# A two-layer hybrid attention and recurrence trunk on one core: output projection's o half scaled as it leaves its slot, value products in other banks, sums' inverses by GpSimd's queue, and several orders of waits and loads

## The chip, the cores and the metric

The program runs on one core of one Trainium2 chip. The time is that of one whole inference step (two layers) in device microseconds, from launch to end; lower is better. Inside the core TensorE (PE) multiplies matrices, VectorE (DVE) and ScalarE (ACT) do elementwise work, GpSimd (POOL) does a few sums and issues DMAs, and SyncE (SP) issues most DMAs. Each engine runs its own instructions in order; semaphores tie them together.

## What is computed

There are 1074 columns of tokens (16 meta tokens, 1024 of a prompt, 32 of a running stream, 2 of padding). Cut to what matters here, a layer of the reference is:

```
z = rmsnorm(x, norm_mix_g) @ w_in                  # -> c_q, c_kv, k_r, x_r, g_r
y = h(x_r) * gelu(g_r)                             # conv, gated recurrence (scan over time)
q = rmsnorm(c_q, q_norm_g) @ w_uq ; ckv = rmsnorm(c_kv) ; kpe = rope(k_r)
k_nope, v = split(ckv @ w_ukv)                     # 8 heads, 64 + 32 rotary columns
o = softmax(mask(q k^T)) v                         # chunk-causal
h = x + concat(rmsnorm(o, attn_out_g), rmsnorm(y, lru_out_g)) @ w_out
x = h + square(relu(rmsnorm(h, norm_mlp_g) @ w_up)) @ w_down
```

## The kernel before

Everything lies transposed: features in the 128 partitions, the 1074 tokens in the free dimension, in three chunks of 358 columns. Each fp32 operand is split into a high and a low part (`xh`, `xl`, `whi`, `wlo`), and each product is three passes of them. A product of 8 blocks of 128 features is so 72 matmuls of 358 columns; one of 4 blocks (the halves of the output projection) is 36.

**Slots and units.** PSUM's banks 0 to 2 and 3 to 5 are two slots. Products are numbered as units `U_...` and take the slots in turn. `take(u)` makes TensorE wait until unit u-2 has been read out of the slot; `READ` says by which semaphore. The sums of squares that the norms need (`sum_of`) go to banks 6 and 7.

**Weights.** 102 blocks of weights a layer come by SP's queue into two buffers `raw0`, `raw1`. `split(b)` stands on ScalarE (which copies `whi`, once the last unit on block b-2 is done) and on VectorE (which subtracts for `wlo`, and counts `w_lo`); TensorE waits for `w_lo`. `load(b)` waits until block b-2 is split.

**The order of a layer.** Four products for the conv's input (`U_XR`), four for the gelu branch (`U_GR`) with the recurrence's gates between them (`gates`), latent, rotary key and query products, `U_UQ` (queries), `U_K`, ten value products of 128 keys each (`U_V`), with the row maxima of head 0 between them, then 8 heads of 19 steps. After them the output projection: 8 units `U_OY` for the y half, then 8 units `U_OO` for the o half, then 4 groups of 16 MLP units. All orders of the five engines are written out by hand; semaphores count per layer.

**Attention.** The scores of step gi need the shifted maxima of their head (`mt`, high and low), which DMAs put into rows of `qe` or `qo`: SP those of the prompt (`aug`), GpSimd those of the few other tokens (`few_shifts`, `aug_few`). `low_parts` (GpSimd) makes the low halves. The softmax sums leave by `srow`, go through DRAM to 16 partitions (`comp`), are inverted by VectorE (`invert`), go back through DRAM and are spread over 64 partitions each (`rc`); `divide(j)` multiplies two heads' o by them. For the last pair this happens while the y half runs.

**The output projection.** `add_y(i)` adds unit `U_OY[i]` to x and frees its slot. The root mean square of o (`rs`) comes from squares made by ScalarE and added by GpSimd (`sum_squares`), summed by TensorE after `U_OY[4]`, then `root` (ScalarE) and `rstd` (VectorE, a reciprocal). Before the change each `o[j]` is multiplied by `rs`, its high half `oh` made by ScalarE and its low half `ol` by VectorE, and only then do the products of the o half start.

## Time and profile before

| | |
|---|---|
| runs | 2770.68 us median of 3 (2768.52 to 2771.31) |
| the profiled execution's own time | 2772.09 us |
| its span, first to last instruction | 2769.9 us |
| mean granted TensorE clock | 0.987 |
| busy: PE / DVE / ACT / POOL | 96% / 47% / 29% / 12% |
| DMA, mean | 52 GB/s |

A busy engine is one with an instruction in flight. The granted clock is a share of TensorE's full speed; 1.00 is 2.4 GHz, and about 0.5 is 1.2 GHz.

### The profile page before, as it was taken

The numbers are of one execution on the slowest core, as the hardware profiler recorded it, in microseconds if no ns is written. First come the engines' busy times: TensorE is split into PE (matmuls) and PEld (weight loads), VectorE is DVE, ScalarE is ACT, GpSimd is POOL, SyncE is SP. The second block draws the span as 40 slices with busy tenths as digits, with TensorE's granted clock in tenths as the row PEclk, the third lists the DMA queues.
The fourth block names the chain that finished last, engine by engine and source line by source line (L and its number), as shares of the span: only waits on it lengthen the run. The fifth ranks groups of instructions, "written<-read, shape, count | busy, mean of one in ns | idle before, by whom it ended". The sixth has DMA issues, their size and how long they took to land.

```text
span 2769.9 us, 37058 instructions
## 1 busy us (share of the span) xinstructions
PE 2668.4 (96%) x15742; PEld 2570.7 (93%) x15742; DVE 1297.4 (47%) x1425; ACT 811.4 (29%) x1240; POOL 327.9 (12%) x192
## 2 busy tenths in 40 slices
PE   6999999999999999999989999999999999999996
PEld 5999977899999999999989998778999999999995
DVE  5899667463223223223368995665632222221323
ACT  3254255442112112022214434552320120210221
POOL 0024144120000000000201223421200000000001
PEclk9999999999999999999999999999999999999998
DMA  3112101211111111111221121012111111111111
GB/s 122 54 61 65 56 16 34 80 46 46 46 46 46 45 41 46 46 47 54 79 73 54 54 80 32 10 41 94 46 46 40 45 46 46 47 43 42 46 46 64
DMA packets 43409, 143.57 MB, mean 52 GB/s; under 512 B 8256, under 2 KB 9376, under 8 KB 43248
## 3 DMA queue, kind: packets, MB, share of 16 engines
q1 hardware_dynamic: 38432, 128.65, 14.2%
q0 software_dynamic: 3232, 6.99, 0.7%
q10 hardware_dynamic: 1584, 5.54, 0.5%
q8 instruction: 132, 2.16, 0.3%
q14 instruction: 29, 0.24, 0.0%
HBM read 127.37 MB, written 11.44 MB: 50 GB/s over the span
## 4 chain that ended last, share of the span: by engine, by line
PE 91%; DVE 5%; DMA 1%; issue 1%; ACT 1%; SPq 0%; POOL 0%; DVEq 0%; POOLq 0%; ACTq 0%
PE ps L786 55%; PE ps L562 22%; PE ps L722 5%; PE ps L737 4%; PE ps L671 1%; PE ps L696 1%; PE ps L607 1%; PE ps L576 1%; DVE wlo L1166 1%; DVE cql L1183 1%; DVE rs L1170 0%; DVE t L1170 0%; DMA fg<-in_fgain 0%; DVE xall L1519 0%; DVE o L1539 0%
## 5 line engine op out<-in xcount | busy, mean ns | idle before, releaser
L1562 DVE TENSOR_TENSOR wlo<-raw,whi 128x1024 fp32r<-128x1024 f32 x126 | 154.4, 1226 | 930.2 <-ACT whi L1101 930.1
L1101 ACT ACTIVATE whi<-raw 128x1024 fp32r<-128x1024 f32 x126 | 133.6, 1060 | 993.2 <-PE ps L786 993.1
L786 PE MATMUL ps<-xmh,whi 128*128 128x358 f32 x1536 | 336.2, 327 | 2.8 <-issue 2.8
L786 PE MATMUL ps<-fl,whi 128*128 128x358 f32 x1536 | 337.3, 327 | 0.0
L786 PE MATMUL ps<-xml,whi 128*128 128x358 f32 x1536 | 336.8, 327 | 0.0
L786 PE MATMUL ps<-fh,wlo 128*128 128x358 f32 x1536 | 336.5, 327 | 0.0
L786 PE MATMUL ps<-fh,whi 128*128 128x358 f32 x1536 | 336.2, 327 | 0.0
L786 PE MATMUL ps<-xmh,wlo 128*128 128x358 f32 x1536 | 335.5, 326 | 0.0
L786 PEld LDWEIGHTS ps<-xmh,whi 128*128 128x128 f32 x1536 | 264.3, 189 | 4.0 <-issue 4.0
L786 PEld LDWEIGHTS ps<-fh,wlo 128*128 128x128 f32 x1536 | 266.8, 189 | 0.0
L786 PEld LDWEIGHTS ps<-fh,whi 128*128 128x128 f32 x1536 | 266.3, 189 | 0.0
L786 PEld LDWEIGHTS ps<-fl,whi 128*128 128x128 f32 x1536 | 265.8, 189 | 0.0
L786 PEld LDWEIGHTS ps<-xmh,wlo 128*128 128x128 f32 x1536 | 265.7, 189 | 0.0
L786 PEld LDWEIGHTS ps<-xml,whi 128*128 128x128 f32 x1536 | 264.5, 189 | 0.0
L562 PE MATMUL ps<-xgh,whi 128*128 128x358 f32 x768 | 170.5, 330 | 16.5 <-DVE wlo L1166 9.4
L1439 DVE TENSOR_REDUCE mxp<-ps 64x1 f32<-64x64 f32 (+11 forms) x384 | 141.2, 372 | 62.7 <-PE ps L671 55.9
L562 PE MATMUL ps<-xgl,whi 128*128 128x358 f32 x768 | 170.2, 330 | 0.0
L562 PE MATMUL ps<-xgh,wlo 128*128 128x358 f32 x768 | 169.4, 329 | 0.0
L830 ACT ACTIVATE whi<-raw 128x1024 fp32r<-128x1024 f32 (+3 forms) x76 | 70.7, 931 | 282.2 <-PE ps L562 249.6
L1572 DVE TENSOR_TENSOR fl<-msq,fh 128x1074 fp32r<-128x1074 f32 x64 | 81.8, 1278 | 147.4 <-ACT fh L1110 147.4
L562 PEld LDWEIGHTS ps<-xgh,whi 128*128 128x128 f32 x768 | 133.6, 192 | 17.1 <-DVE wlo L1166 9.6
L1166 DVE TENSOR_TENSOR wlo<-raw,whi 128x1024 fp32r<-128x1024 f32 (+3 forms) x76 | 101.9, 1341 | 73.6 <-ACT whi L830 73.1
(273 smaller groups left out, 3925.4 us busy)
## 6 DMA issues: line engine op xcount, KB each, us to landing
raw<-in_wst SPq DMA_DIRECT2D x204, 512.0 KB, 3.3
xall<-in_xT SPq DMA_DIRECT2D x11, 537.0 KB, 7.5
x_scratch<-xall POOLq DMA_DIRECT2D x8, 537.0 KB, 3.5
out_yT<-xall SPq DMA_DIRECT2D x8, 537.0 KB, 3.3
rc<-sum_scratch SPq DMA_DIRECT2D x16, 268.0 KB, 4.0
xall<-in_xT ACTq DMA_DIRECT2D x5, 537.0 KB, 5.7
xall<-x_scratch ACTq DMA_DIRECT2D x5, 537.0 KB, 6.4
ra<-qr SPq DMA_DIRECT2D x16, 134.2 KB, 2.4
```

Of the source, the lines that this page charges most:

```text
L562: mm = nc.tensor.matmul(dst(q), wt, r(q), start=(k == 0 and i == 0), stop=(k == n - 1 and i == 2))
L576: nc.tensor.matmul(ps[:, 6 + q, :], ones[:, :], tile[:, 512 * q:512 * q + 512], start=True, stop=True)
L607: mm = nc.tensor.matmul(dst(q), wt, (XH if b == "h" else XL)[k](q), start=(k == 0 and i == 0), stop=(k == 7 and i == 2))
L722: mm = nc.tensor.matmul(ps[0:65, bank, c0:c0 + n], v[:, v0:v0 + 65], p_tile(gk)[:, 0:n], start=(k in FIRST), stop=(k in LAST))
L737: mm = nc.tensor.matmul(ps[:, gi % 3, 0:n], ks[e][0 if a == "h" else 1][rows, k0:k0 + P], qs[e][0 if c == "h" else 1][rows, q0:q0 + n], st ...
L786: mm = nc.tensor.matmul(ps[:, 3 * slot_of(u) + q, 0:CH], wt, (rh if c == "h" else rl)[kk](q), start=(kk == 0 and i == 0), stop=(kk == 7 an ...
L830: nc.scalar.activation(whi[b % 2][:, 0:n], raw[b % 2][:, 0:n], ACT.Copy).then_inc(S["w_hi"], 1)
L1101: nc.scalar.activation(whi[b % 2][:, :], raw[b % 2][:, :], ACT.Copy).then_inc(S["w_hi"], 1)
L1166: V.tensor_tensor(wlo[b % 2][:, 0:n], raw[b % 2][:, 0:n], whi[b % 2][:, 0:n].bitcast(F32), ALU.subtract).then_inc(S["w_lo"], 1)
L1439: ins = V.reduce_max(mxp[lo_:hi_, tile, part:part + 1], ps[lo_:hi_, max_bank(h, s), c0:c0 + n], AX_X)
L1562: V.tensor_tensor(wlo[b % 2][:, :], raw[b % 2][:, :], whi[b % 2][:, :].bitcast(F32), ALU.subtract).then_inc(S["w_lo"], 1)
L1572: V.tensor_tensor(fl[k][:, :], msq[:, :], fh[k][:, :].bitcast(F32), ALU.subtract).then_inc(S["f_lo"], 1)
```

## The change

- Loads: blocks 2 and 3 are loaded before the small tables of a layer; in layer 0 they are also split before the norm's root and reciprocal. TensorE waits for the constants only at the first sum.
- VectorE reads `U_GR[1]` out before it splits block 7. The reciprocal for y's norm and the memsets of the key's helper rows stand behind the low halves of the query latent.
- Value products write banks 3 to 5, not 0 to 2, and so wait for the third key product's copy, not the fourth's. `kslot_hi(1)` moves from ScalarE to VectorE, `qn_hi(1)` and the load of the exponential's table into the value products, `split(30)` to the end of head 0.
- o's halves are made without `rs`. Instead each `U_OO` unit is multiplied by `rs` into `osqt` as it leaves its slot (which frees the slot, `oo_ev`), and a second instruction adds it to x (`res_add`). `add_y(0)` stands behind `divide(3)`.
- The inverses go out and are spread by GpSimd's queue (`spread_inverse`), not by SP's; `rc` lies elsewhere.
- TensorE's MLP loop is written out.

Of the diff, what the prediction speaks of (tables of semaphores and two renamed buffers are left out):

```diff
     READ[U_OY[_c]] = ("oy_ev", _c + 1)
-    READ[U_OO + _c] = ("res_add", _c + 1)
+    READ[U_OO + _c] = ("oo_ev", _c + 1)
...
-        rc = place("rc", "X", 4 * TB + 1536 * 8, T)
+        rc = place("rc", "R", 6 * TB, T)
...
-
+                load(2)
+                load(3)
+                if L:
                     sp.wait_ge(S["xg_hi"], L * 8 + 8)
...
-                with sp.Fori(1, 14) as i:
+                with sp.Fori(2, 14) as i:
...
-                            flat = sum_scr[2 * j:2 * j + 2, :].rearrange("a (r n) -> (a r) n", r=8)
-                            sp.dma_start(comp[:, :], flat).then_inc(S["sum_in"], 16)
-                            w("inv", j + 1)
-                            sp.dma_start(flat, comp[:, :]).then_inc(S["inv_out"], 16)
-                            w("inv_out", 16 * (j + 1))
-                            for e in range(2):
-                                sp.dma_start(rc[half(e), 0:TOK], sum_scr[2 * j + e:2 * j + e + 1, :].to_broadcast([64, TOK]))\
-                                    .then_inc(S["inv_in"], 16)
+                            if j:
+                                w("inv_out", 16 * j)
+                            sp.dma_start(comp[:, :], flat_sums(j)).then_inc(S["sum_in"], 16)
...
-                    if n > 1 or L:
+                    if n == 1 and L == 0:
+                        pe.wait_ge(S["const_in"], 48)
+                    else:
                         pe.wait_ge(S["root"], L * PER["root"] + n - 1)
...
-                pe.wait_ge(S["const_in"], 48)
...
                     if t < 3:
-                        w("kf", 4)
+                        w("kf", 3)
                     else:
                         w("v_ev", t - 2)
...
-                            mm = nc.tensor.matmul(ps[:, t % 3, :], (ckvh if a == "h" else ckvl)[k][:, c0:c0 + P],
+                            mm = nc.tensor.matmul(ps[:, 3 + t % 3, :], (ckvh if a == "h" else ckvl)[k][:, c0:c0 + P],
...
-                w("v_ev", 10)
+                w("kf", 4)
...
+                        if gk == 0:
+                            w("v_ev", 10)
...
-                mlp_group(0, True)
-                with pe.Fori(1, GROUPS) as gg:
-                    mlp_group(gg, False)
+                for gg in range(GROUPS):
+                    mlp_group(gg, gg == 0)
...
                     nc.scalar.activation(chunks(xr[0][:, CW - 1:CW - 1 + T]), slot(U_XR[0]), ACT.Copy).then_inc(S["xr_raw"], 1)
+                    split(3)
                 root(SUM_MIX, rs, DM)
-                split(3)
+                if L:
+                    split(3)
...
-                    nc.scalar.activation(dst, ps[:, t % 3, :].rearrange("p (h d) -> p h d", h=NH), ACT.Copy).then_inc(S["v_ev"], 1)
+                    nc.scalar.activation(dst, ps[:, 3 + t % 3, :].rearrange("p (h d) -> p h d", h=NH), ACT.Copy).then_inc(S["v_ev"], 1)
+                    if t == 2:
+                        w("qr", 2)
+                        qn_hi(1)
+                    if t == 4:
+
+                        nc.scalar.activation(spw[:, 4:8], spw[:, 0:4], ACT.Exp, scale=-1.0)
                     if t == 6:
                         shift_hi(0)
-                kslot_hi(1)
-                w("qr", 2)
-                qn_hi(1)
-                split(30)
...
+                    if h == 0 and i == MX_END + 2:
+                        split(30)
...
+                def o_high(j):
+
                     w("o", j + 1)
+                    nc.scalar.activation(oh[j][:, :], o[j][:, :], ACT.Copy, scale=col(V_AG + j)).then_inc(S["o_hi"], 1)
+
+                def o_square(j):
+
                     if j >= 2:
                         w("o_sum", j - 1)
                     nc.scalar.activation((osqt if j else osq)[:, :], o[j][:, :], ACT.Square).then_inc(S["o_sq"], 1)
+
+                w("pv", NH * NP)
+                for j in range(3):
+                    o_high(j)
+                    o_square(j)
+                split(31)
+                o_high(3)
+                o_square(3)
                 split(32)
                 root(SUM_O, rs, ATT)
                 split(33)
-                for j in range(4):
-                    w("o_n", j + 1)
-                    nc.scalar.activation(oh[j][:, :], o[j][:, :], ACT.Copy, scale=col(V_AG + j)).then_inc(S["o_hi"], 1)
-                    if j == 0:
-                        split(34)
+                split(34)
...
-                    nc.scalar.activation((rs if m else msq)[:, :], x[m], ACT.Square).then_inc(S["xm_sq"], 1)
+                    nc.scalar.activation((osq if m else msq)[:, :], x[m], ACT.Square).then_inc(S["xm_sq"], 1)
...
                 split(2)
-                rstd(rs, 1)
+                if L == 0:
+                    split(3)
+                rstd(rs, SUM_MIX)
                 xr_out(0)
                 xr_out(1)
-                split(3)
+                if L:
+                    split(3)
...
+                scaled(U_GR[1], g[1], rs, "gr_ev")
                 split(7)
-                scaled(U_GR[1], g[1], rs, "gr_ev")
...
-                link(V.tensor_copy(kpe[:, OWN2:PAST_B], kpe[:, STREAM:TOK]))
-                link(V.memset(kpe[32:64, PAST_A:KW], 0.0))
-                V.memset(kpe[32:33, :], 1.0)
-                V.memset(kpe[96:97, :], 1.0).then_inc(S["kpe_ones"], 1)
+                V.tensor_copy(kpe[:, OWN2:PAST_B], kpe[:, STREAM:TOK]).then_inc(S["kpe_copy"], 1)
...
-                rstd(t3, SUM_Y)
                 cq_low(2)
                 cq_low(3)
                 scaled(U_CQ[5], cq[5], rs, "cq_ev")
                 cq_low(4)
                 cq_low(5)
                 split(22)
+                w("kpe_copy", 1)
+                link(V.memset(kpe[32:64, PAST_A:KW], 0.0))
+                V.memset(kpe[32:33, :], 1.0)
+                V.memset(kpe[96:97, :], 1.0).then_inc(S["kpe_ones"], 1)
 
                 w("kv_out", 32)
                 for c in range(2):
                     w("ckv_hi", c + 1)
                     lo(ckvl[c][:, :], ckv[c][:, :], ckvh[c][:, :], "ckv_lo")
                 split(23)
+                rstd(t3, SUM_Y)
...
-                load_hi(0)
+                load_q(0)
...
+                    if s == 7:
+                        load_q(1)
...
-                            load_hi(h + 1)
+                            if h:
+                                load_q(h + 1)
+                            load_k(h + 1)
                             if h == 0:
+                                kslot_hi(1)
                                 kslot_lo(1)
-                                split(30)
+                        if h == 0 and i == 15:
+                            split(30)
...
+                def o_low(j):
+
+                    w("o_hi", j + 1)
+                    w("o_sq", j + 1)
+                    lo(ol[j][:, :], o[j][:, :], oh[j][:, :], "o_lo", col(V_AG + j))
+
+                for j in range(3):
+                    o_low(j)
+                divide(3)
                 add_y(0)
-                divide(3)
                 add_y(1)
                 split(31)
+                o_low(3)
                 add_y(2)
                 split(32)
                 add_y(3)
@@ -1535,21 +1584,19 @@
                 rstd(rs, SUM_O)
                 split(33)
                 add_y(5)
-                for j in range(4):
-                    V.tensor_tensor(o[j][:, :], o[j][:, :], rs[:, :], ALU.mult).then_inc(S["o_n"], 1)
-                    if j == 0:
-                        split(34)
                 add_y(6)
-                for j in range(4):
-                    w("o_hi", j + 1)
-                    lo(ol[j][:, :], o[j][:, :], oh[j][:, :], "o_lo", col(V_AG + j))
+                split(34)
                 add_y(7)
                 split(35)
                 for m in range(8):
                     if m and m % 2 == 0:
                         split(35 + m // 2)
-                    w("oy_ev", 8)
-                    add_up(U_OO + m, m, "res_add")
+                    if m == 0:
+                        w("oy_ev", 8)
+                        w("o_sum", 3)
+                    scaled(U_OO + m, osqt, rs, "oo_ev")
+                    w("oo_ev", m + 1)
+                    V.tensor_tensor(x[m], x[m], osqt[:, :], ALU.add).then_inc(S["res_add"], 1)
                     w("xm_hi", m + 1)
...
+                def spread_inverse(j):
+
+                    w("inv", j + 1)
+                    pool.dma_start(flat_sums(j), comp[:, :]).then_inc(S["inv_out"], 16)
+                    w("inv_out", 16 * (j + 1))
+                    for e in range(2):
+                        pool.dma_start(rc[half(e), 0:TOK], sum_scr[2 * j + e:2 * j + e + 1, :].to_broadcast([64, TOK])).then_inc(S["inv_in"], 16)
+
                 few_shifts(0)
                 for h in range(1, NH):
                     low_parts(h)
+                    if h % 2 == 1 and h >= 3:
+                        spread_inverse((h - 3) // 2)
                     few_shifts(h)
+                spread_inverse(3)
                 sum_squares(osq[:, :], osqt[:, :], 4, "o_sq", "o_sum")
-                sum_squares(msq[:, :], rs[:, :], 8, "xm_sq", "xm_sum")
```

On VectorE, where attention ends and the y half starts, there stood before (`xall` is x, `ps` PSUM; in brackets what is waited for):

```order
L1464 RECIPROCAL comp<-comp 16x134 [waits sum_in]
L1519 TENSOR_TENSOR xall<-xall,ps 128x1074 [waits mm,x_in5]
L1470 MEMSET o_151 128x2 [waits o_ev,inv_in]
L1471 TENSOR_TENSOR o_151<-o_151,rc 128x1072
L1519 TENSOR_TENSOR xall<-xall,ps 128x1074 [waits mm,x_in6]
L1166 TENSOR_TENSOR wlo_54<-raw_50,whi_52 128x1024 [waits w_hi]
L1519 TENSOR_TENSOR xall<-xall,ps 128x1074 [waits mm,x_in7]
```

and there stands now:

```order
L1497 RECIPROCAL comp<-comp 16x134 [waits sum_in]
L1201 SCALAR_TENSOR_TENSOR ol_164<-o_148,vecs,oh_160 128x1074 [waits o_sq,o_hi]
L1201 SCALAR_TENSOR_TENSOR ol_165<-o_149,vecs,oh_161 128x1074 [waits o_sq,o_hi]
L1201 SCALAR_TENSOR_TENSOR ol_166<-o_150,vecs,oh_162 128x1074 [waits o_sq,o_hi]
L1503 MEMSET o_151 128x2 [waits o_ev,inv_in]
L1504 TENSOR_TENSOR o_151<-o_151,rc 128x1072
L1559 TENSOR_TENSOR xall<-xall,ps 128x1074 [waits mm,x_in5]
L1559 TENSOR_TENSOR xall<-xall,ps 128x1074 [waits mm,x_in6]
L1184 TENSOR_TENSOR wlo_54<-raw_50,whi_52 128x1024 [waits w_hi]
L1201 SCALAR_TENSOR_TENSOR ol_167<-o_151,vecs,oh_163 128x1074 [waits o_sq,o_hi]
```

The first addition that frees a slot (wait `x_in5`) stood ahead of the last division and now stands behind three low halves of o and that division.

On VectorE, in the o half, a unit was one addition from PSUM, and is now a product into `osqt` and an addition. Before:

```order
L1519 TENSOR_TENSOR xall<-xall,ps 128x1074 [waits mm,oy_ev]
L1183 SCALAR_TENSOR_TENSOR xml_179<-xall,vecs,xmh_171 128x1074 [waits xm_hi]
L1519 TENSOR_TENSOR xall<-xall,ps 128x1074 [waits mm,oy_ev]
L1183 SCALAR_TENSOR_TENSOR xml_180<-xall,vecs,xmh_172 128x1074 [waits xm_hi]
L1166 TENSOR_TENSOR wlo_53<-raw_49,whi_51 128x1024 [waits w_hi]
```

Now:

```order
L1194 TENSOR_TENSOR osqt<-ps,rs 128x1074 [waits mm,o_sum,oy_ev]
L1599 TENSOR_TENSOR xall<-xall,osqt 128x1074 [waits oo_ev]
L1201 SCALAR_TENSOR_TENSOR xml_179<-xall,vecs,xmh_171 128x1074 [waits xm_hi]
L1194 TENSOR_TENSOR osqt<-ps,rs 128x1074 [waits mm]
L1599 TENSOR_TENSOR xall<-xall,osqt 128x1074 [waits oo_ev]
L1201 SCALAR_TENSOR_TENSOR xml_180<-xall,vecs,xmh_172 128x1074 [waits xm_hi]
L1184 TENSOR_TENSOR wlo_53<-raw_49,whi_51 128x1024 [waits w_hi]
```

Each unit has one more instruction between TensorE's end and `xm_hi`.

On ScalarE, at attention's start, before (`v` are the value products' copies, `pd` the first exponentials):

```order
L1029 ACTIVATE v<-ps 128x8x64 [waits mm] x6
L1016 ACTIVATE mt<-ps 10x128 [waits mxt]
L1029 ACTIVATE v<-ps 128x8x64 [waits mm] x3
L987 ACTIVATE koh<-kpe 64x1296
L995 ACTIVATE qo<-qn_116 64x1074 [waits qn,qr]
L830 ACTIVATE whi_51<-raw_49 128x1024 [waits mm,raw0]
L1046 ACT_TABLE_LOAD [waits s]
L1046 ACTIVATE pd_138<-ps 16x16 [waits p_zero]
```

Now:

```order
L1036 ACTIVATE v<-ps 128x8x64 [waits mm] x2
L1002 ACTIVATE qo<-qn_116 64x1074 [waits qn,qr]
L1036 ACTIVATE v<-ps 128x8x64 [waits mm] x2
L1042 ACT_TABLE_LOAD
L1042 ACTIVATE spw<-spw 128x4
L1036 ACTIVATE v<-ps 128x8x64 [waits mm] x2
L1023 ACTIVATE mt<-ps 10x128 [waits mxt]
L1036 ACTIVATE v<-ps 128x8x64 [waits mm] x3
L1055 ACTIVATE pd_138<-ps 16x16 [waits s,p_zero]
```

The copies `koh` and `whi_51` are gone from this place, and `qo` and the table's load stand among the value copies.

## Rows read from the trace of the kernel before

**Rows 1.** The page's first part: busy time (share of the span) and instructions.
```profile
PE 2668.4 (96%) x15742; PEld 2570.7 (93%) x15742; DVE 1297.4 (47%) x1425; ACT 811.4 (29%) x1240; POOL 327.9 (12%) x192
```

**Rows 2.** TensorE's waits over the span: us in total, times, longest.
```profile
PE ps L607 <- DMA fg<-in_fgain: 17.7, 1, 17.7
PE ps L562 <- DVE wlo L1166: 11.2, 3, 9.4
PE ps L562 <- DVE ol L1183: 8.8, 2, 4.4
PE ps L562 <- issue: 7.0, 1, 7.0
...
PE ps L562 <- DVE g L1176: 4.5, 2, 2.3
PE ps L562 <- DVE cql L1183: 4.1, 4, 1.6
PE ps L786 <- issue: 2.8, 4, 0.9
PE ps L737 <- DMA qo<-mt: 2.1, 2, 1.6
```

**Rows 3.** The chain that ended last, piece by piece: start us, us, what.
```profile
17.75 26.66 PE ps L607 x144
...
55.72 50.22 PE ps L562 x288
...
514.12 29.87 PE ps L562 x180
...
568.02 50.10 PE ps L562 x288
...
1191.58 190.28 PE ps L786 x1152
...
1414.56 50.07 PE ps L562 x288
```

**Rows 4.** Timeline of VectorE, layer 0: start us, us, line, operation, tiles.
```profile
8.62 1.22 DVE L1143 TENSOR_TENSOR wlo<-raw,whi 128x1024 fp32r<-128x1024 f32 x1
...
251.74 6.86 DVE L1170 RECIPROCAL t<-t 128x1074 f32<-128x1074 f32 x1
...
521.99 0.98 DVE L1464 RECIPROCAL comp<-comp 16x134 f32<-16x134 f32 x1 [7.97 <-DMA comp<-sum_scratch]
...
529.36 1.27 DVE L1471 TENSOR_TENSOR o<-o,rc 128x1072 f32<-128x1072 f32 x1 [5.09 <-issue]
...
598.97 2.44 DVE L1166 TENSOR_TENSOR wlo<-raw,whi 128x1024 fp32r<-128x1024 f32 x1 [0.60 <-ACT whi L830]
```

**Rows 5.** Timeline of GpSimd in layer 0's output projection.
```profile
598.06 2.26 POOL L1619 TENSOR_TENSOR msq<-msq,rs 128x1074 f32<-128x1074 f32 x1 [2.79 <-ACT rs L1091]
```

**Rows 6.** Timeline of TensorE, attention's start (both layers).
```profile
331.06 0.47 PE L696 MATMUL ps<-whi,ckvh 128*128 128x512 f32 x1 [0.96 <-ACT kf L1007]
...
352.50 1.38 PE L722 MATMUL ps<-pd,v 128*65 128x336 f32 x2 [2.42 <-ACT pd L1046]
...
1706.57 0.55 PE L737 MATMUL ps<-qe,keh 97*128 97x336 f32 x2 [1.29 <-DMA qe<-mt]
```

**Rows 7.** Stretch after attention's start: PE, PEld, DVE, ACT, POOL busy, PEclk, DMA, GB/s.
```profile
352.00:358.40 6.40, 5.90 (x19) 4.84 (x20) 3.78 (x9) 2.10 (x12) 6.28 (x3) 0.51 0.00 0
```

**Rows 8.** Timeline of VectorE, layer 1: shifts' low half; last division.
```profile
1701.80 0.28 DVE L1450 SCALAR_TENSOR_TENSOR mt<-ps,mt 10x128 fp32r<-10x128 f32 x1 [2.47 <-ACT mt L1016]
...
1886.92 1.27 DVE L1471 TENSOR_TENSOR o<-o,rc 128x1072 f32<-128x1072 f32 x1 [5.87 <-issue]
```

**Rows 9.** Timeline of ScalarE, attention's start in layer 0.
```profile
350.62 1.28 ACT L1046 ACT_TABLE_LOAD   x1
```

**Rows 10.** DMA issues: queue, KB each, median us from issue to landing.
```profile
rc<-sum_scratch SPq DMA_DIRECT2D x16, 268.0 KB, 4.0
...
qo<-mt POOLq DMA_DIRECT2D x8, 0.2 KB, 2.4
```

More of the change, by code:

```diff
@@ L152 @@
 Y_AT = [3, 6, 9, 14]
-DVE_CHAIN = 87
+DVE_CHAIN = 86
 VTILES = [P * t for t in range(10)]
@@ L1426, in load_hi, with load_k, kslot_hi @@
                         V.memset(qs[1][0][32:33, :].bitcast(F32), 0.0)
-                    for dst, src, rows in slot_parts(h)[1:]:
-                        ins = V.tensor_copy(dst[0][rows, :], src[rows, :])
-                    ins.then_inc(S["q_hi"], 1)
+                    dst, src, rows = slot_parts(h)[1]
+                    V.tensor_copy(dst[0][rows, :], src[rows, :]).then_inc(S["q_hi"], 1)
+                def load_k(h):
+                    if h == 0:
+                        w("kf", 1)
+                    if h == 1:
+                        w("mm", U_V + 10)
+                    if h == 2:
+                        w("kf", 4)
+                    if h >= 2:
+                        w("s", (h - 1) * NP)
+                    dst, src, rows = slot_parts(h)[2]
+                    V.tensor_copy(dst[0][rows, :], src[rows, :]).then_inc(S["k_hi"], 1)
+                def kslot_hi(e):
+                    V.tensor_copy(ks[e][0][KEY_ROWS[e], :], kpe[KEY_ROWS[e], :]).then_inc(S["kslot_hi"], 1)
                 def max_bank(h, s):
@@ L1537, in _ @@
                 add_y(5)
-                for j in range(4):
-                    V.tensor_tensor(o[j][:, :], o[j][:, :], rs[:, :], ALU.mult).then_inc(S["o_n"], 1)
-                    if j == 0:
-                        split(34)
                 add_y(6)
-                for j in range(4):
-                    w("o_hi", j + 1)
-                    lo(ol[j][:, :], o[j][:, :], oh[j][:, :], "o_lo", col(V_AG + j))
+                split(34)
                 add_y(7)
```

26 lines of the change are left out of this document (13 added, 13 removed).

## The prediction

> **What bounds the kernel now.** I read the page's busy line first [rows 1]. TensorE is busy 96% of the span, VectorE 47%, the rest less. The reader is to see that only what leaves TensorE idle, or runs it at its lower clock, can give time back. The list of its waits comes next [rows 2]: it names each idle piece with its releaser, and the edits each sit on one of them. The chain [rows 3] prices the clock. The MLP's 1152 matmuls take 190.28 us, so one takes 0.1652 us at full speed. The 288 matmuls behind the long wait for `wlo` take 50.22 us and not 47.6, the 288 at layer 1's start 50.07 us, and the 288 of the o half 50.10 us: each long stall costs about 2.5 us more, in matmuls at a lower granted clock. The stretch after attention's start shows that clock directly: 0.51 over 6.4 us, of which TensorE is busy 5.90 [rows 7], which is the 1.2 GHz level.
>
> **The change part by part** (gains negative).
>
> *A, the constants.* TensorE's first wait ends with the DMA of `fg` at 17.75 us [rows 2, 3], though products need only the first `wlo`, done at 8.62+1.22 = 9.84 [rows 4]. With the wait moved to the first sum: −7.9. A block of both units takes 18 × 0.1652 = 2.97 us, and VectorE's low halves and squares (1.2 to 1.3 us each, like the split) fit below that, so the gain isn't eaten by supply.
>
> *B, blocks 2 and 3 in layer 0.* Their split ends late, behind small loads and the 6.86 us reciprocal [rows 4]; TensorE waits 9.4 us [rows 2] and then loses 2.6 to the clock (50.22−47.6, [rows 3]). The early load and split take both away: −12.0. Late next is the norm's scale, root plus 6.86 us, then two scaled readings. The first two units end at 9.84+26.66 = 36.5; sums and root about 1.5, 6.86, and two readings of 1.27 make 47.4, and the fourth unit can start when the third ends, 36.5+11.9 = 48.4. So it just fits; if not, up to 6.9 comes back.
>
> *C, gates.* `g` is waited for twice, 4.5 in all [rows 2]. The wait left is the copy before it, which I put at 0.65 each: −3.2.
>
> *D, layer 1's loads.* One wait of 7.0 called "issue" [rows 2], in front of the 50.07 [rows 3]: with the loads ahead of the small tables both go, 7.0+2.5: −9.5.
>
> *E, query latent.* Low halves `cql` cost 4.1 in 4 waits and the two short `wlo` waits 11.2−9.4 = 1.8 [rows 2]: 5.9. With the reciprocal (6.86) and the memsets behind them, the reciprocal now pushes the queries' own scale back by its length; I leave 1.2 a layer for that: −3.5. Bounds: −5.9 and, with 6.86 late in each layer less what TensorE has queued (two units, over 20 us), nothing.
>
> *F, values and attention's start.* In layer 0 the first value product waits 0.96 for `kf`, the first p·v 2.42 for `pd`, which stands behind the 1.28 us table load [rows 6, 9]; scores wait for the shifts, 1.29 for `qe` in layer 1 [rows 6] and 1.6 and 0.5 for `qo` [rows 2]. Together about 0.96+1.6+2.42 = 5.0 a layer. The other banks need one key copy less, and the table is loaded long before. The shifts stay: the low half is made at 1701.80 [rows 8] and the scores that read it begin at 1706.57 [rows 6], nearly 5 us in a small transfer, which is not shortened; some 1.2 stays idle. So −3.8, and without the two stalls the 5.90 busy us at 0.51 [rows 7] become about 3.2: −2.7. Two layers: −13.0. Bounds: −7.6 (the clock falls anyway) and −15.4.
>
> *G, the MLP loop written out.* The four waits "issue" at L786 go [rows 2]: −2.8.
>
> *H, the output projection.* This one costs. Removed: the wait for `ol`, 4.4 a layer [rows 2], and the 2.5 of clock behind it [rows 3]. Added in front: `add_y(0)` frees the slot that the third y unit wants. The y half begins at 514.12 [rows 3], so that unit could start 2 × 36 × 0.1652 = 11.9 later, at 526.0. But `add_y(0)` now stands behind the last division. The inverse ends at 521.99+0.98 = 522.97, the division begins at 529.36 [rows 4], after a write to DRAM and a spread of 4.0 [rows 10]. Ahead of it stands also `o_low(2)`, which waits for the third square; that waits for GpSimd's first sum, and GpSimd is held by `spread_inverse(3)` until the inverse is out (about 526.3). Sum 2.26 [rows 5], square 1.1, low half 1.3: 530.9; division 1.27 and addition 1.27: 533.4. TensorE stalls 7.4 and pays 2.5 of clock. All of VectorE's later work of the y half is queued behind it, but only slots make TensorE wait. In layer 1 the division starts 1.0 later against the half's own start (1886.92, [rows 8]).
>
> Added in the o half: VectorE has per pair of units two products, two additions (1.27 each), two low halves (1.34) each after 1.26 of ScalarE's copy, and one split: 2 × 5.14 + 2.44 = 12.7, plus 1.2 if the new addition too runs while GpSimd adds. TensorE needs 11.9. The first MLP unit waits for the seventh addition: 3 × 13.9 + 2 × 1.27 = 44.2 after the first unit's end, TensorE is there after 7 × 5.95 = 41.6: a stall of 2.6 and about 1.2 of clock. The 2.44 is a row: the same split takes 1.22 at the start and 2.44 while GpSimd's 2.26 us addition runs [rows 4, 5]. I extend that to the new addition, whose operands both lie in SBUF too; without it 12.7 gives a stall below 0.1 and 3.8 less a layer, which is the lower bound. The Trainium skill ("SBUF — State Buffer", Who interferes with whom) states that VectorE's second port pair is shared with GpSimd under an exclusive lock. By that rule the addition would be slowed as well, and the sum is as above.
>
> Layer 0: −4.4−2.5+7.4+2.5+2.6+1.2 = +6.8; layer 1: +7.8. H = +14.6. Above: +5 a layer if GpSimd's queue is slower than SP's.
>
> *I, inverses by GpSimd's queue.* For pairs 0 to 2 `few_shifts` of an odd head now stands behind two transfers of 268 KB, 4.0 us each, where its own takes 2.4 [rows 10]. The shifts of a head are made well before its scores; I take 0. Bounds: −2.1 (the `qo` waits go) and 6 heads (three a layer) × (4.0−2.4) = +9.6. The Trainium skill ("DMA: Bandwidth & Descriptors", SWDGE vs HWDGE vs iDMA) says that DMAs issued by GpSimd have their descriptors built by software, with a first byte after about 1 us against 0.6. By that, an estimate, each of the three hops comes 0.4 later, which no row here shows; it speaks against this edit, and the sum goes without it.
>
> Sum: −7.9−12.0−3.2−9.5−3.5−13.0−2.8+14.6 = −37.3. The profiled execution took 2772.09, so 2734.8; the median of the runs is 1.4 lower, so **2733**.
>
> **The rivals.**
> *R1, the division is in time.* If the inverse comes back before 521 (VectorE is free earlier) and the addition isn't slowed, H loses its price. That the division waited 5.09 for nothing but transfers [rows 4] speaks against it: the inverses can't start before the last sums. Gives 2733−14.6 = 2718.
> *R2, one front gain isn't had.* The norm's scale in layer 0 comes late (B's 6.9), or the clock stays low where it was low (2 × 2.7): 12 more, 2745. For it: the reciprocal's 6.86 leaves no slack by my count.
> *R3, GpSimd's queue is slow.* +9.6 by I and 5 in each output projection: 2753. Against it: before, its small transfers landed in 2.4 [rows 10].
> *R4, the other side, one mechanism:* `few_shifts` of the odd heads comes after the transfers and the scores wait for it. It ends slower than before once each of the 6 heads costs over 37.3/6 = 6.2. With both 4.0 us transfers in series (8.0) less 3.0 of slack, 5, and 2.5 of clock, each costs 7.5, 45 in all: 2778. Against it: the transfers before ran side by side, and the scores' longest wait for shifts is 1.6 in a whole span [rows 2].
>
> **How the numbers follow.** Forecast 0.65 (2726 to 2741 by itself: the bounds of F, and 2 × 3.8 of H), R1 0.12, R2 0.12, R3 0.06, R4 0.05. The range leaves out the lowest part of R1 and R4: 2720 to 2753. A measurement of this kernel tells 0.2%, 5.5 us, from no change. All but R4 lie over 15 us below: faster 0.93, same 0.02, slower 0.05.
>
> **What would show it.** TensorE's first matmul near 9.8 us; no wait for `wlo` of 9 us; layer 1 beginning without the "issue" of 7; a granted clock near 1 at attention's start. Against that a new wait for the addition L1559 of about 7 us in the y half, twice, the division ahead of it, and a wait for L1599 of 2 to 3 us before the MLP; GpSimd's transfers of `rc` at 4 to 5 us. The prediction is wrong if the first wait reappears elsewhere in layer 0 (scale late), if the y half has no stall, or if waits for `qo` or `qe` appear at heads 3, 5 and 7.

## The result and the profile after

The changed kernel takes 2753.92 us (median of 6 runs, 2748.0 to 2759.34), the kernel before 2770.04 us (2768.49 to 2771.31): a ratio of 0.994, interval 0.9925 to 0.9955. It is faster, by 16 us where 37 were forecast, and its median lies 0.9 above the range. Its runs are spread over 11 us, those of before over 3, and two of its six, at 2748, lie inside the range. The profiled execution took 2753.91, its span is 2752.0.

The page's busy line shows 6.4 us less of TensorE [rows 1], 26 more of VectorE and 13 more of GpSimd:

```profile
PE 2662.0 (97%) x15742; PEld 2566.6 (93%) x15742; DVE 1323.3 (48%) x1435; ACT 807.6 (29%) x1240; POOL 341.2 (12%) x216
```

TensorE's waits after, in the form of [rows 2]:

```profile
PE ps L563 <- DVE xall L1559: 20.4, 2, 10.6
PE ps L609 <- DVE wlo L1161: 10.1, 1, 10.1
PE ps L743 <- DMA qo<-mt: 8.1, 6, 2.3
PE ps L563 <- DVE wlo L1184: 5.9, 4, 2.0
PE ps L792 <- issue: 5.8, 2, 2.9
PE ps L806 <- POOL msq L1774: 4.7, 1, 4.7
PE ps L675 <- DVE mxp L1472: 3.0, 2, 1.7
```

The first wait is 10.1 in place of 17.7, and those of 9.4, 7.0 and 4.4 are gone. Five others have come: for the addition L1559 in the y half, for `qo` at six places in place of two, for weights behind the moved reciprocal (two of 2.0 in the row of 5.9), for the MLP's slot (L792), and for the row maxima. The six places of `qo` are the starts of heads 3, 5 and 7 in both layers (388.8, 430.3 and 471.9 us in layer 0), which the prediction had named as a sign of being wrong. The chain shows the pieces behind the first ones at full clock (47.65 for 288 matmuls, where [rows 3] has 50.22), and the MLP in one piece:

```profile
10.09 26.54 PE ps L609 x144
38.51 47.65 PE ps L563 x288
...
618.48 748.28 PE ps L792 x4536
```

TensorE's timelines of the two executions give the end of each stage, and so a table that sets each stage's change against the prediction's steps. All are us; the last two columns are changes of the stage's length.

| stage ends with | before | after | forecast | measured |
|---|---|---|---|---|
| L0, first product behind the first `xcs` block (A, B, C) | 111.24 | 89.92 | −21.5 | −21.3 |
| L0, last query unit's end (E) | 314.51 | 293.77 | −1.75 | +0.6 |
| L0, first p·v (F, idle) | 352.50 | 327.18 | −3.8 | −4.6 |
| L0, y half starts (F, clock; I) | 514.12 | 490.71 | −2.7 | +1.9 |
| L0, second MLP unit (H) | 631.68 | 618.30 | +6.8 | +10.0 |
| L0, the MLP ends (G) | 1381.86 | 1366.76 | −1.4 | −1.7 |
| L1, the same (D, C) | 1469.91 | 1443.68 | −11.1 | −11.1 |
| L1, last query unit's end (E) | 1673.20 | 1649.05 | −1.75 | +2.1 |
| L1, first p·v (F, idle) | 1711.18 | 1682.88 | −3.8 | −4.2 |
| L1, y half starts (F, clock; I) | 1870.65 | 1844.77 | −2.7 | +2.4 |
| L1, second MLP unit (H) | 1988.13 | 1972.50 | +7.8 | +10.3 |
| end (G) | 2769.94 | 2751.99 | −1.4 | −2.3 |

The front of both layers is as forecast. The whole is 17.95 shorter and not 37.3. What is missing lies in attention (9.7), the query latent (6.2) and the output projection (5.7); the idle part of F and G gave 2.4 more than forecast.

**The y half.** VectorE's timeline, from the inverse on:

```profile
499.31 0.98 DVE L1497 RECIPROCAL comp<-comp 16x134 f32<-16x134 f32 x1 [8.70 <-DMA comp<-sum_scratch]
500.22 2.47 DVE L1201 SCALAR_TENSOR_TENSOR ol<-o,vecs,oh 128x1074 fp32r<-128x1074 f32 x2
507.55 3.20 DVE L1201 SCALAR_TENSOR_TENSOR ol<-o,vecs,oh 128x1074 fp32r<-128x1074 f32 x1 [4.86 <-ACT osqt L1088]
510.68 1.26 DVE L1504 TENSOR_TENSOR o<-o,rc 128x1072 f32<-128x1072 f32 x1
...
511.98 2.46 DVE L1559 TENSOR_TENSOR xall<-xall,ps 128x1074 f32<-128x1074 f32 x2
```

GpSimd's, of the same time (issues and sums):

```profile
500.58 0.52 POOL L1752 DMA_DIRECT2D sum_scratch<-comp  x1 [31.74 <-DVE comp L1497]
503.14 1.03 POOL L1755 DMA_DIRECT2D rc<-sum_scratch  x2 [2.03 <-DMA sum_scratch<-comp]
504.24 2.08 POOL L1666 TENSOR_TENSOR osq<-osq,osqt 128x1074 f32<-128x1074 f32 x1
507.53 2.08 POOL L1666 TENSOR_TENSOR osq<-osq,osqt 128x1074 f32<-128x1074 f32 x1 [1.21 <-ACT osqt L1088]
```

The third unit could start at 502.7, two units of 5.95 after 490.7; it starts at 513.39, when the first of the two L1559 is done. It is the sequence that the prediction wrote down, 3.2 us longer (10.6 for 7.4). The inverse ends 9.6 us after the half's start, where 8.9 was counted on. GpSimd's first sum begins 3.95 behind the inverse's end (500.29 to 504.24), for 3.3. And the third low half takes 3.20 us and not 1.3, while GpSimd's second sum runs: it ends 1.1 behind that sum's end at 509.61, which is nearly its whole length alone (1.23). That is 1.9 of the 3.2. In layer 1 it takes 2.84, and the stall is 9.8.

**Attention's start.** VectorE, the low half of the key's rows for head 1:

```profile
325.55 0.83 DVE L1462 CAST koh<-kpe 64x1296 fp32r<-64x1296 f32 x1
326.41 3.68 DVE L1199 TENSOR_TENSOR kol<-kpe,koh 64x1296 fp32r<-64x1296 f32 x1
330.02 3.41 DVE L1472 TENSOR_REDUCE mxp<-ps 128x1 f32<-128x80 f32 x11
```

GpSimd at the same time:

```profile
325.69 3.04 POOL L1720 TENSOR_TENSOR qo<-qn,qo 64x1074 fp32r<-64x1074 f32 x1 [2.62 <-DVE koh L1458]
```

In the kernel before, the same low half had run ahead of GpSimd's `low_parts`, which began at 349.59:

```profile
348.43 1.50 DVE L1181 TENSOR_TENSOR kol<-kpe,koh 64x1296 fp32r<-64x1296 f32 x1 [0.25 <-ACT koh L987]
```

Eleven parts of row maxima then stand queued, and TensorE waits for them (the 1.7 above).

**The query latent.** VectorE after the low halves:

```profile
251.72 6.86 DVE L1188 RECIPROCAL t<-t 128x1074 f32<-128x1074 f32 x1
258.62 4.84 DVE L1406 TENSOR_TENSOR g<-g,t 128x1074 f32<-128x1074 f32 x4
263.37 0.95 DVE L1184 TENSOR_TENSOR wlo<-raw,whi 128x768 fp32r<-128x768 f32 x1
264.24 6.86 DVE L1188 RECIPROCAL rs<-rs 128x1074 f32<-128x1074 f32 x1
...
274.70 0.95 DVE L1184 TENSOR_TENSOR wlo<-raw,whi 128x768 fp32r<-128x768 f32 x1
```

The reciprocal for y's norm and the product behind it now stand in front of the queries' own reciprocal, which starts at 264.24 (258.98 in run e3 below, where the first one is back in its old place). The split behind it ends at 275.65; TensorE has waited 2.04 for it.

### The profile page after: what moved, and what is told of

Read it like the earlier page. It is cut to its first block, busy times and chain, and to the rows that moved or that the text cites. A ratio compares the mean times of both kernels' runs of the same rounds, so it can differ in the third digit from the quotient of the medians.

```text
span 2752.0 us, 36936 instructions
## 1 busy us (share of the span) xinstructions
PE 2662.0 (97%) x15742; PEld 2566.6 (93%) x15742; DVE 1323.3 (48%) x1435; ACT 807.6 (29%) x1240; POOL 341.2 (12%) x216
## 4 chain that ended last, share of the span: by engine, by line
PE 89%; DVE 6%; DMA 2%; issue 1%; ACT 1%; POOL 0%; SPq 0%; DVEq 0%; ACTq 0%; POOLq 0%
PE ps L792 55%; PE ps L563 21%; PE ps L728 4%; PE ps L743 4%; PE ps L675 2%; PE ps L700 1%; PE ps L609 1%; DVE wlo L1184 1%; DMA qo<-mt 1%; PE ps L579 1%; DVE xall L1599 1%; DVE t L1188 0%; DVE rs L1188 0%; DVE osqt L1194 0%; DMA comp<-sum_scratch 0%
## 5 line engine op out<-in xcount | busy, mean ns | idle before, releaser
L792 PE MATMUL ps<-xmh,whi 128*128 128x358 f32 x1536 | 337.0, 328 | 5.8 <-issue 5.8
L792 PE MATMUL ps<-xml,whi 128*128 128x358 f32 x1536 | 338.0, 328 | 0.0
L792 PE MATMUL ps<-fl,whi 128*128 128x358 f32 x1536 | 337.3, 327 | 0.0
L792 PE MATMUL ps<-fh,wlo 128*128 128x358 f32 x1536 | 336.5, 327 | 0.0
L792 PE MATMUL ps<-xmh,wlo 128*128 128x358 f32 x1536 | 336.4, 327 | 0.0
L792 PE MATMUL ps<-fh,whi 128*128 128x358 f32 x1536 | 336.2, 327 | 0.0
L792 PEld LDWEIGHTS ps<-xmh,whi 128*128 128x128 f32 x1536 | 265.4, 190 | 6.3 <-issue 6.3
L792 PEld LDWEIGHTS ps<-fh,wlo 128*128 128x128 f32 x1536 | 266.8, 189 | 0.0
L792 PEld LDWEIGHTS ps<-xmh,wlo 128*128 128x128 f32 x1536 | 266.7, 189 | 0.0
L792 PEld LDWEIGHTS ps<-fh,whi 128*128 128x128 f32 x1536 | 266.3, 189 | 0.0
L792 PEld LDWEIGHTS ps<-fl,whi 128*128 128x128 f32 x1536 | 265.8, 189 | 0.0
L792 PEld LDWEIGHTS ps<-xml,whi 128*128 128x128 f32 x1536 | 265.5, 189 | 0.0
L563 PEld LDWEIGHTS ps<-xgh,wlo 128*128 128x128 f32 x768 | 132.9, 189 | 0.0
```

Of the source, the lines that this page charges most:

```text
L563: mm = nc.tensor.matmul(dst(q), wt, r(q), start=(k == 0 and i == 0), stop=(k == n - 1 and i == 2))
L792: mm = nc.tensor.matmul(ps[:, 3 * slot_of(u) + q, 0:CH], wt, (rh if c == "h" else rl)[kk](q), start=(kk == 0 and i == 0), stop=(kk == 7 an ...
```

## The experiments

All are timed in five rounds beside the kernel before, which took 2769.7 to 2771.0 there. The interval of each ratio is 0.0013 to 0.0015 on either side, some 4 us, as it is for the changed kernel. The difference between two variants is so known to some 6 us; what is smaller rests on the traces.

**e1: the inverses by SP's queue.** `spread_inverse` is taken out of GpSimd's program:

```diff
                             sp.dma_start(comp[:, :], flat_sums(j)).then_inc(S["sum_in"], 16)
+                            w("inv", j + 1)
+                            sp.dma_start(flat_sums(j), comp[:, :]).then_inc(S["inv_out"], 16)
+                            w("inv_out", 16 * (j + 1))
+                            for e in range(2):
+                                sp.dma_start(rc[half(e), 0:TOK], sum_scr[2 * j + e:2 * j + e + 1, :].to_broadcast([64, TOK]))\
+                                    .then_inc(S["inv_in"], 16)
...
-                    if h % 2 == 1 and h >= 3:
-                        spread_inverse((h - 3) // 2)
```

> The changed kernel (2753.9) with the inverses written and spread by SP's queue again, GpSimd's queue free of them. Theory 1 (what stands behind the transfers in GpSimd's queue is late: the shifts of heads 3, 5 and 7, and the first sum of squares, on which the third low half of o and so the last division and the first addition hang): waits for qo fall from 8.1 us to 2 to 3, and the y half's two stalls from 10.6 and 9.8 to about 8 each; 2743, range 2740 to 2747. Rival (those waits come from the earlier start of attention, whatever queue is used): 2752 to 2756, waits for qo still about 8.

Measured: 2741.2 us (2740.18 to 2741.96), ratio 0.9892 (0.9877 to 0.9907). Its waits:

```profile
PE ps L567 <- DVE xall L1563: 11.7, 2, 5.9
...
PE ps L747 <- DMA qo<-mt: 3.4, 4, 1.5
```

and SP's timeline after the inverse:

```profile
497.94 0.31 SPq L516 DMA_DIRECT2D sum_scratch<-comp  x1
499.46 1.15 SPq L519 DMA_DIRECT2D rc<-sum_scratch  x2
```

Theory 1 holds, and the y half's stalls fell further than it said, to 5.9 each. Two things do it. GpSimd's first sum no longer stands behind the inverse, and the third low half is done before the spread lands; GpSimd's timeline:

```profile
495.20 2.09 POOL L1670 TENSOR_TENSOR osq<-osq,osqt 128x1074 f32<-128x1074 f32 x1 [27.32 <-ACT osqt L1092]
498.50 5.02 POOL L1670 TENSOR_TENSOR osq<-osq,osqt 128x1074 f32<-128x1074 f32 x1 [1.22 <-ACT osqt L1092]
```

The sum begins 6.3 us after the y half's start (488.93), where it began 13.5 after it in the changed kernel. And the round trip is shorter. From the issue of the write to that of the spread SP needs 1.52 us (497.94 to 499.46), GpSimd 2.56 (500.58 to 503.14), but this is GpSimd's longest of eight. Its other seven are 1.92 to 2.02, SP's eight 1.34 to 1.57: 0.6 longer as a rule, half of it until the write lands and half between landing and the next issue (0.28 for 0.02). Counted from the half's start in layer 0, the spread has landed 1.9 earlier in e1, and the division then starts at once (504.18), where in the changed kernel it stood another 2.8 behind the third low half: together the 4.7 by which the stall is shorter. The whole edit gives 12.7 us in the medians and 11.8 in the profiled spans.

In attention it isn't the issue that is late. For head 3 GpSimd stood free 0.46 us and waited for the shifts' low half (the bracket of the row below), but what it then issues lands later, behind the two transfers of 268 KB. The changed kernel's timeline of GpSimd, and its DMA issues, with 3.3 beside the 2.4 of [rows 10]:

```profile
382.13 1.05 POOL L1755 DMA_DIRECT2D rc<-sum_scratch  x2 [1.38 <-DMA sum_scratch<-comp]
383.64 0.51 POOL L1746 DMA_DIRECT2D qo<-mt  x1 [0.46 <-DVE mt L1483]
```

```profile
qo<-mt POOLq DMA_DIRECT2D x8, 0.1 KB, 3.4
qo<-mt POOLq DMA_DIRECT2D x8, 0.2 KB, 3.3
```

In e1 both rows are back at 2.4. The same transfers of 268 KB run there too, on SP's queue; at head 1, where none runs, the small ones land after 1.5 to 1.6 in all four kernels (before, changed, e1, i1).

**i1: the queue alone, in the kernel before.** The same move the other way, nothing else changed.

> The kernel before with the inverses written and spread by GpSimd's queue, nothing else. Theory 1 (shifts of heads 3, 5 and 7 stand about 1 us later behind the transfers, and the hops take 1.8 us longer, which the second addition of the y half waits for): 2770.6 plus 4 to 5 in attention and 3.6 in the y halves, 2778, range 2775 to 2782. Rival (only the changed kernel's earlier start makes the queue matter): 2769 to 2773.

Measured: 2781.76 us (2778.88 to 2785.22), ratio 1.0043 (1.0029 to 1.0056). Theory 1, the kernel is slower, by 12.1. Waits:

```profile
PE ps L736 <- DMA qo<-mt: 6.7, 6, 2.3
PE ps L561 <- DVE xall L1518: 5.1, 2, 2.6
```

The first was 2.1 in two [rows 2]; the second, 0.9 in one before, is the y half's second addition behind the last division:

```profile
531.52 3.12 DVE L1470 TENSOR_TENSOR o<-o,rc 128x1072 f32<-128x1072 f32 x1 [5.60 <-issue]
```

GpSimd's second sum runs from 531.43 to 533.51, since the sums stand behind the inverse here too, and the division beside it takes 3.12 (2.99 in layer 1) and not 1.27 [rows 4]. 4.6 and 4.2 of waiting are 8.8; the stages of attention are 5.0 longer in the two layers, those of the projection 6.7. The profiled spans differ by 9.9, and what is over in the medians stays open.

**e5: the division ahead of the third low half.**

```diff
-                for j in range(3):
+                for j in range(2):
                     o_low(j)
                 divide(3)
                 add_y(0)
+                o_low(2)
```

> The changed kernel with the last division and the first addition of the y half ahead of o's third low half, on VectorE. Theory 1 (the stall is set by the third low half, which waits for GpSimd, 2.4 us behind the arrival of the spread inverse): stalls of about 8 in place of 10.6 and 9.8; 2749, range 2747 to 2751. Rival (the spread inverse itself is what comes last): stalls unchanged, 2754.

Measured: 2749.12 us (2748.24 to 2752.98), ratio 0.9922 (0.9908 to 0.9935). Waits for the addition: 18.4 in two, the longest 9.5, for 20.4 and 10.6. The gain of the median, 4.8, is as expected but within its uncertainty; the traces show only 2 us less of waiting and a span 1.1 shorter, and why: the division itself now runs beside GpSimd's sum and takes 2.92, not 1.26.

```profile
507.84 2.92 DVE L1504 TENSOR_TENSOR o<-o,rc 128x1072 f32<-128x1072 f32 x1 [5.64 <-issue]
```

So giving up the place behind the third low half gives 1 us a layer: what the low half no longer costs, the division beside GpSimd's sum takes back in part. The place behind the division, with its way through DRAM, is the rest.

**e6: each addition where its unit ends.**

```diff
-                for j in range(3):
-                    o_low(j)
-                divide(3)
-                add_y(0)
-                add_y(1)
-                split(31)
-                o_low(3)
-                add_y(2)
+                o_low(0)
+                add_y(0)
+                o_low(1)
+                add_y(1)
+                o_low(2)
+                divide(3)
+                split(31)
+                add_y(2)
+                o_low(3)
```

> The changed kernel with the additions of the y half on VectorE placed between the low halves of o, so that each stands where its unit ends, and the last division behind the second addition. Theory 1 (the y half's whole loss is the position of the first addition): no stall over 1 us in the y half and no slow clock behind it, y half 49.5 us in place of 61.9; 2729, range 2727 to 2734. Rival (something else of the y half, the norm of o or the loads of x, holds the o half back as soon as the additions do not): the stall moves to the o half and half or less is gained, 2740 or more.

Measured: 2731.11 us (2727.47 to 2732.09), ratio 0.9854 (0.9839 to 0.9869). Theory 1: the row for `xall` is gone from TensorE's waits and none takes its place. The y half lasts from 493.95 to 543.13, 49.2 us, for 61.9 in the changed kernel and 53.9 before. All of the stall was the position of the additions, and it goes although the inverses are still GpSimd's. From the y half's start to the second MLP unit the two layers take 113.49 and 115.10, for 117.56 and 117.48 before: the rewritten projection is shorter than the old one, once its additions stand in time.

**g1: the whole output projection of before.** The order that the kernel before has there: the first addition first, o multiplied by `rs` before it is split; the inverses still by GpSimd.

> The changed kernel with the whole output projection of before (o multiplied by its scale before it is split, the first addition first), the inverses still by GpSimd's queue. Theory 1 (the new output projection as ordered costs 10.0 and 10.3 us, from the y half's start to the second MLP unit): 2753.9 less 20.3, 2733.6, plus up to 4 because the second addition stands behind a division that is late by the queue: 2732 to 2738. Rival (the prediction's 14.6, the rest being the clock's accidents): 2739 or more.

Measured: 2739.81 us (2738.98 to 2742.7), ratio 0.9894 (0.9879 to 0.9909). Theory 1's number was too low; the rival's range holds it. The waits say what was left out:

```profile
PE ps L563 <- DVE ol L1194: 8.8, 2, 4.4
...
PE ps L563 <- DVE xall L1552: 5.1, 2, 2.6
```

With the old order the late division still stops TensorE, at the second addition, as in i1. So of the 20.3 us that the stages after attention lost, some 14 belong to the rewritten projection (2753.9 to 2739.8; 15.1 by these stages in the traces), close to the 14.6 of step H, and the rest to the queue. The two don't simply add up, since the queue costs more behind the new order than behind the old: with SP's queue, in e1, the same stages are 12.5 longer than before, so that the queue's share in the changed kernel is 7.7.

**e3: the query latent's order of before.**

```diff
                 split(21)
+                rstd(t3, SUM_Y)
                 cq_low(2)
...
-                rstd(t3, SUM_Y)
```

and the three memsets of `kpe` behind the copy again.

> The changed kernel with the reciprocal for y's norm and the memsets of the key's rows back ahead of the query latent's low halves. Theory 1 (the move only pushed the wait on: the reciprocal now delays the queries' scale and the weights behind it, 2.04 us and a lower clock in each layer): the three short waits of 3.0 us a layer come back, the one of 2.04 goes; 2751, range 2749 to 2754. Rival (the prediction's step E, the move saves 1.75 a layer): 2757.

Measured: 2751.73 us (2749.87 to 2752.32), ratio 0.9929 (0.9916 to 0.9943). The medians' difference of 2.2 is within their intervals; the trace decides. The stretches from the first `xcs` block to the last query unit, 203.85 and 205.37 us in the changed kernel, are 203.41 and 203.35 here, against 203.27 and 203.29 before: the loss is gone. Step E is refuted. Of layer 1's loss in the changed kernel 1.5 us is TensorE's lower clock behind the wait: the executions of g1 and b2, with the same order there, are without it and take 203.81 and 203.83.

**e4: the copy of the key's rows on ScalarE.** `kslot_hi(1)` behind the value copies, as before.

> The changed kernel with the copy kslot_hi(1) on ScalarE behind the value products' copies again, not on VectorE at attention's start. Theory 1 (VectorE's copy and the low half behind it, 3.68 us beside GpSimd's low_parts where it took 1.50, make the row maxima late: waits of 1.7 and 1.3 for mxp): waits for mxp gone, 2753.9 less 3, 2751. Rival (the low half is as slow wherever the copy stands, because GpSimd works at that time): waits for mxp at least 1 each, 2754.

Measured: 2749.68 us (2749.22 to 2753.61), ratio 0.9922 (0.9909 to 0.9936). The trace is on the rival's side for about half of it:

```profile
PE ps L675 <- DVE mxp L1473: 1.6, 2, 1.1
```

The wait falls from 3.0 to 1.6 and not to nothing, since the low half still takes 3.06 beside GpSimd. Its profiled span is the changed kernel's to 0.2 us (2751.8), so the median's 4 us are not shown to be its doing.

**f1: the early loads alone, in the kernel before.** Steps A, B and D: blocks 2 and 3 first, the early split in layer 0, the constants awaited at the first sum.

> The kernel before with the early loads of blocks 2 and 3 in both layers, the early split in layer 0 and the late wait for the constants, nothing else. Theory 1 (steps A, B and D of the prediction were right, and what they gain is kept to the end): 2770.2 less 7.7, 12.1 and 9.6, 2740.8, range 2738 to 2744; the first matmul at 10, layer 1's wait of 7.0 gone. Rival (attention and the y half start earlier against their loads and transfers and give part of it back): 2746 or more.

Measured: 2743.96 us (2743.14 to 2745.27), ratio 0.9902 (0.9887 to 0.9918), 27.1 less where 29.4 was expected. That is theory 1, at the edge of its range. The three long waits are gone from its list, but for the 10.2 until the first weights, and TensorE starts at 10.17. So three small edits alone beat the whole change by 10 us: the rest of it, as ordered, loses time.

**b2: the MLP waits for its slot only.** On top of e6:

```diff
-                        if k < 2:
+                        if k < 2 and first:
+                            w("oo_ev", 7 + k)
+                        elif k < 2:
                             pe.wait_ge(S["res_add"], L * PER["res_add"] + gg * 8 + (7 + k))
```

> The changed kernel with the y half's additions placed where the units end, and the first two MLP units waiting only until their slot has been read out (the product into osqt), not for the addition to x. Theory 1 (the 2.9 us before the MLP in each layer, and 1.4 of clock behind it, come from a wait for an addition that the slot no longer needs): 2731.1 less 8.6, 2722.5, range 2720 to 2726. Rival (VectorE is behind by then, and TensorE waits the same time for the low half of x, the seventh or eighth, instead): 2729 or more, with a wait for xml in place of the one called issue.

Measured: 2721.88 us (2721.31 to 2722.65), ratio 0.9821 (0.9808 to 0.9835). The number is theory 1's, its size by the trace isn't: the wait is 1.6 in each layer and not 0, 1.3 less, which is the addition alone. VectorE is behind with the product before it too.

```profile
PE ps L794 <- issue: 3.2, 2, 1.6
```

From the y half's start to the second MLP unit the traces differ by 1.3 in layer 0 (112.19 for 113.49) and 1.7 in layer 1 (113.35 for 115.10). The other 4.7 of the 7.7 between the two spans lie elsewhere, 3.3 of them in layer 0's attention, where e6's profiled run met the lower clock.

**b1 and h1: the parts together.**

> The changed kernel with the y half's additions placed where the units end, the inverses by SP's queue, the query latent's order of before, and the copy kslot_hi(1) on ScalarE. Theory 1 (the parts are separate waits of TensorE and add up): from 2731.1 with the additions alone, 3.3 less in attention by the queue, 2.5 less by the latent's order, 3.0 less by the row maxima: 2722, range 2719 to 2726. Rival (TensorE's clock in attention falls for other reasons, and what one wait gives back another takes): 2727 or more.

Measured: 2721.97 us (2716.97 to 2722.7), ratio 0.9819 (0.9806 to 0.9833): theory 1. Its runs fall in two groups, two at 2717 and 2718, three at 2722 to 2723.

> b1_combined (additions in time, SP's queue, latent order of before, ScalarE's copy) with the first two MLP units waiting for their slot alone. Theory 1 (the waits are separate; b2_slot_wait's trace shows 1.3 us less of waiting in each layer, the rest of the wait being the product ahead of the addition): 2722.0 less 3 to 6, 2717.5, range 2715 to 2720. Rival (the wait there is given back by the low half of x): 2721 to 2723.

Measured: 2713.53 us (2713.16 to 2714.59), ratio 0.9797 (0.9783 to 0.981). It is below even theory 1's range and the fastest of all: 40 us under the changed kernel, 56 under the one before. The 8.4 us under b1's median are mostly b1's slower group: the two profiled spans differ by 2.5 (2714.9 and 2712.4). Waits for `qo` are 3.1 in it, for the additions 0.9.

## Why the prediction was wrong

The step that failed is I, the queue of the inverses, which was put at nothing and cost 12 us. Beside it E had the wrong sign, and a wait for `mxp` had no step.

- **A, B, C, D** were right: −21.3 and −11.1 against −21.5 and −11.1, and f1 shows A, B and D by themselves. The norm's scale came in time for the fourth unit, as counted. **F's** idle part (−4.6, −4.2 against −3.8) and **G** (−4.0 against −2.8) were slightly better than forecast.
- **I failed, and it is the largest error.** "I take 0" had to be 12: i1 shows 12.1 in the kernel before, e1 12.7 in the changed one. In attention the bound of 9.6 had the right mechanism (the shifts land behind the 268 KB transfers; 3.3 for 2.4), and the price as a stretch of 4.0−2.4 a head was even generous, 6.0 more of waiting being measured, 4.7 of which e1 takes away. What it left out is the way of the inverse in the y half. There the division stands between TensorE and a slot, and GpSimd's sums, held until the inverse is out, fall on VectorE's work: with the projection of before that costs 2.1 of waiting a layer, with the new one 4.7 and 4.0.
- The Trainium skill ("DMA: Bandwidth & Descriptors", SWDGE vs HWDGE vs iDMA) had spoken against this edit, and the sign was right. Of the 0.4 a hop that the prediction estimated from that page's figures, the traces show 0.3 for the write (it lands after 1.65 for 1.35) and 0.26 each before the write's and the spread's issue; the spreads themselves take 4.0 on either queue. By that alone the inverse comes some 0.8 later, much less than the stalls grew.
- **Rival R3** had the time, 2753, with 9.6+10 for the queue, and was given 0.06. That its number is met is partly luck: the queue costs 12, and what fills up its 20 is E and `mxp`, which it didn't have.
- **E failed in sign:** −3.5 forecast, +2.7 measured, e3 gives it back. The new wait was put at 1.2 a layer and is 2.04; of the short waits that the move should remove, 0.43 and the 0.90 for `wlo` stayed in each layer. Without the 1.5 of lower clock in layer 1, which g1 and b2 don't have, it is still +1.1.
- **H** was right in mechanism, too small in two terms. Stalls of 10.6 and 9.8 stood where 7.4 and 8.4 were forecast, 2.9 before the MLP where 2.6 was. The low half beside a GpSimd sum took 3.20 and the one of the key's rows 3.68, which the prediction didn't price. That agrees with the rule it cited from the Trainium skill ("SBUF — State Buffer", Who interferes with whom), which holds for more instructions than the one it was applied to. In the o half a pair of units takes VectorE 13.8 (574.11 to 587.93), where 13.9 was forecast, but the reason was half of it: of the 1.2 beyond 12.7, 0.6 is one slowed addition (1.86 for 1.28, in 6 of the 16), and 0.6 is VectorE's wait for ScalarE's copy of the weights.
- **F's clock** came back at full level (1.00 in the stretch that had 0.51 [rows 7]); TensorE's busy time in attention fell by 2.4 a layer, where 2.7 was forecast. But TensorE idles 4.4 and 4.8 more there. Besides I's `qo` that is `mxp`, 3.0 in all, a new wait that no step named. e4 gives 1.4 of it to the copy `kslot_hi(1)`; the rest comes with the low half, which falls beside GpSimd's work wherever the copy stands. Together they turned the −2.7 of each attention into +1.9 and +2.4.

So the 19.4 that the table misses are attention's 9.7 (nearly all of it the 6.0 for `qo` and the 3.0 for `mxp`), E's 6.2 and 5.7 in the projection, where the queue's 7.7 stands against an H that without it measured 12.5 for 14.6; less 2.4 by F and G.

## What to carry to other kernels

Before a transfer is moved to another queue, list who else's small transfers follow on that queue and who waits for them: the queue move was nearly free in bytes and cost 12 us, as much as step B, the best single one, was to gain. Look also at what the issuing engine does next: while it waits for the inverse, its own sums wait with it. A piece that frees a PSUM slot belongs where its unit ends; putting a 1.3 us addition behind a round trip through DRAM stopped TensorE for 10 us a layer, and setting the additions back in time gained 22.8. When a long instruction is moved off one path, look at what follows in the new place: here it met a second one of its kind.

## What was unexpected of the hardware

- A write to DRAM and the spread behind it were issued 0.6 us further apart by GpSimd (1.92 to 2.02 in seven of eight, 2.56 once) than by SP (1.34 to 1.57). Half is the landing:

```profile
sum_scratch<-comp POOLq DMA_DIRECT2D x8, 8.4 KB, 1.6
```

```profile
sum_scratch<-comp SPq DMA_DIRECT2D x8, 8.4 KB, 1.3
```

  The first is the changed kernel's, the second e1's. A transfer of 0.2 KB issued by GpSimd landed after some 3.3 us behind two of 268 KB on its own queue, after 2.4 beside the same two on SP's, and after 1.5 to 1.6 with neither.
- VectorE's instructions with two operands in SBUF took 2.0 to 2.6 times as long beside a GpSimd operation: 3.68 and 3.06 for 1.50, 3.20 for 1.23, 2.92 for 1.26. It goes the other way too: in e1 GpSimd's second sum, which began while VectorE's three low halves ran (3.73 in all, unslowed), took 5.02 for 2.09.
- With waits of 1 to 3 us strewn through attention the granted clock fell in some executions and not in others of like kernels. The same two stretches (PE, PEld, DVE, ACT, POOL, then PEclk) of e6, and of the changed kernel, whose program is the same there:

```profile
325.00:345.00 20.00, 17.71 (x92) 13.87 (x93) 15.15 (x31) 7.64 (x34) 9.62 (x3) 0.91 0.03 12
389.00:431.00 42.00, 39.38 (x215) 30.87 (x215) 26.82 (x65) 19.72 (x76) 19.30 (x13) 0.96 0.03 10
```

```profile
325.00:345.00 20.00, 17.78 (x101) 14.15 (x102) 15.41 (x32) 9.18 (x37) 10.63 (x5) 1.00 0.04 13
389.00:431.00 42.00, 40.21 (x228) 31.52 (x228) 28.02 (x66) 21.71 (x78) 18.81 (x14) 1.00 0.06 15
```

e6's attention took 3.2 us more. It fits the wider spread of the changed kernel's runs (11 us against 3, and 1.4 in h1, whose waits are shorter), and these go with the mean granted clock: 0.991 in the run of 2748.0, 0.990 in that of 2753.9, 0.987 in that of 2759.3. That the short waits bring the lower clock about is not shown.
